# Tile 0 alone through the pooling mixer and its first routing, with tile 1's rows moved behind the first gathers, and another order of the buffer ring

## The reference

```python
# the pooling mixer of layer 1
m = multiscale_pool(h @ w_in)               # four bands of averages over the tokens, minus h
m = einsum('btgc,gce->btge', m, w_grp)      # four groups of 256 channels
y = (m * scale) @ w_out
xs = layer_norm(alpha * xs + g1 * y)        # per token; also after each expert layer

# PEER, for each block of 128 tokens ("tile"), 8 heads
q = (h @ wq).reshape(128, 8, 2, 128)
s = einsum('nhpd,hpkd->nhpk', q, keys)      # 2 x 128 scores per token and head
top_s, top_i = top_k(s, 16)                 # then the best 16 of 16 x 16 sums
gate = softmax(best_s)
act = gelu(einsum('nd,nhkd->nhk', h, u_tab[idx]))
out = einsum('nhk,nhkd->nd', gate * act, v_tab[idx])
```

## Time and profile before

| | us |
|---|---|
| median of three runs | 2215.3 (2212.99 to 2216.16) |
| the profiled execution, its own time | 2214.42 |
| its span | 2212.6 |
| PE busy | 1827.7 (83%) |
| DVE busy | 1467.5 (66%) |
| ACT busy | 882.3 (40%) |
| POOL busy | 620.3 (28%) |
| share of 16 DMA engines' span, gathers (software_dynamic) | 59.0% |
| the same, other loads (hardware_dynamic) | 22.1% |

### The profile page before, as it was taken

The page is one execution under the profiler, slowest core; times in us unless marked ns, Lnnn a source line. Parts: engine busy times, 40 slices in busy tenths (PEclk is TensorE's granted clock), DMA queues, the critical chain, the costliest instruction groups (busy, mean ns, idle before and its releaser), DMA issues.

```text
span 2212.6 us, 21909 instructions
## 1 busy us (share of the span) xinstructions
PE 1827.7 (83%) x7101; PEld 1097.5 (50%) x7101; DVE 1467.5 (66%) x3019; ACT 882.3 (40%) x2302; POOL 620.3 (28%) x567
## 2 busy tenths in 40 slices
PE   4888999899868687988877877996889888877786
PEld 3757998799656444434322333354434343322222
DVE  6767956955675666677567777525576777677755
ACT  3446433522443234344434444312343444444433
POOL 1160000000000334434354443203244344444441
PEclk9889989998988799999999999997999999999999
DMA  9754757646344599999999999845899999999995
GB/s 369 264 197 146 267 186 296 238 183 248 105 143 145 209 384 416 421 418 421 380 418 422 421 422 421 343 171 218 360 418 420 419 421 421 421 421 421 421 422 247
DMA packets 114690, 723.76 MB, mean 327 GB/s; under 512 B 11504, under 2 KB 13344, under 8 KB 34064
## 3 DMA queue, kind: packets, MB, share of 16 engines
q0 software_dynamic: 74864, 540.30, 59.0%
q1 hardware_dynamic: 39712, 182.07, 22.1%
HBM read 721.24 MB, written 1.08 MB: 326 GB/s over the span
## 4 chain that ended last, share of the span: by engine, by line
PE 40%; DMA 30%; DVE 19%; issue 5%; ACT 5%; POOL 1%; SPq 0%; DVEq 0%; ACTq 0%; POOLq 0%
DMA X<-in_k_uv,EI 15%; PE PS L2020 14%; DMA Z<-in_k_uv,EI 8%; DMA W<-in_peer_wq 5%; PE PS L1997 5%; PE PS L1709 5%; PE PS L1710 4%; PE PS L1711 4%; DVE junk L1696 4%; DVE ACC L1320 3%; DVE WL L1336 2%; PE PS L1797 2%; DMA W<-in_ada_w 2%; PE PS L2073 1%; PE PS L2035 1%
## 5 line engine op out<-in xcount | busy, mean ns | idle before, releaser
L2020 PE MATMUL PS<-X,dg 128*128 128x512 f32 x1372 | 669.1, 623 | 166.6 <-ACT dg L908 160.1
L1696 DVE CUSTOM_DVE_ANT_0 junk<-H,X 128x1024 f32<-128x1024 f32 x343 | 420.0, 1224 | 239.3 <-DMA X<-in_k_uv,EI 229.2
L899 POOL DMA_INDIRECT X<-in_k_uv,EI x343 | 377.8, 1101 | 618.8 <-PE PS L2020 375.7
L2020 PEld LDWEIGHTS PS<-X,dg 128*128 128x128 f32 x1372 | 249.0, 194 | 543.0 <-ACT dg L908 328.0
L908 ACT ACTIVATE CF<-DOT 128x1 f32<-128x1 f32 x512 | 102.2, 200 | 576.8 <-DVE DOT L1696 567.2
L2020 PE MATMUL PS<-Z,dg 128*128 128x512 f32 x504 | 248.0, 625 | 53.0 <-ACT dg L908 52.7
L908 ACT ACTIVATE dg<-CP,CG 128x128 f32<-128x128 f32 x512 | 205.7, 402 | 17.5 <-PE PS L2020 0.7
L1696 DVE CUSTOM_DVE_ANT_0 junk<-H,Z 128x1024 f32<-128x1024 f32 x126 | 154.2, 1224 | 85.7 <-DMA Z<-in_k_uv,EI 76.6
L2020 PEld LDWEIGHTS PS<-Z,dg 128*128 128x128 f32 x504 | 92.0, 195 | 191.0 <-ACT dg L908 115.9
L899 POOL DMA_INDIRECT Z<-in_k_uv,EI x126 | 137.3, 1089 | 142.4 <-PE PS L2020 122.0
L1709 PE MATMUL PS<-XH,WH 128*128 128x256 f32 x592 | 173.6, 293 | 2.4 <-ACT XH L908 1.2
(11 more groups left out here) (298 smaller groups left out, 2642.5 us busy)
## 6 DMA issues: line engine op xcount, KB each, us to landing
W<-in_ada_w SPq DMA_DIRECT2D x50, 1024.0 KB, 6.5
Y<-in_ada_w SPq DMA_DIRECT2D x22, 1024.0 KB, 5.5
W<-in_peer_wq SPq DMA_DIRECT2D x16, 1024.0 KB, 16.2
W<-in_k_ffi SPq DMA_DIRECT2D x13, 1024.0 KB, 6.6
Y<-in_k_ffi SPq DMA_DIRECT2D x9, 1024.0 KB, 5.1
W<-in_ffn_w_out SPq DMA_DIRECT2D x8, 1024.0 KB, 5.4
W<-in_k_win SPq DMA_DIRECT2D x8, 1024.0 KB, 6.1
Y<-in_k_win SPq DMA_DIRECT2D x8, 1024.0 KB, 7.5
```

The source lines that it names most:

```text
L899: e.indirect_dma_start(out=WS[k][:, :], out_offset=None, in_=I[f"k_uv{ly}"][:, :], in_offset=bass.IndirectOffsetOnAxis(ap=EI[t][:, j:j + 1 ...
L1696: e.tensor_tensor_reduce(junk, H[:, t, :], d[:, 0:D], 1.0, 0.0, ALU.mult, ALU.add, DOT[:, j:j + 1]).then_inc(v_dot, 1)
L2020: p = e.matmul(PS[:, 2 * t + q, :], dgb[n % 4][:, :], d[:, D + q * 512:D + (q + 1) * 512], start=(j == 0), stop=(j == 127))
```

## The change

The pooling bands and groups are made tile by tile, each matmul 128 tokens wide instead of 256, and bands and groups alternate. The output matmuls `po` are split by tile: tile 0's come before its `rn`, and tile 1's (`("po", 1)`) directly behind head 0's score matmuls of layer 1. Tile 1's bands and groups stand between `rn` of tile 0 and `tt` of tile 0. In both layers, `rn`, `tt` and `h` of tile 1 become three pieces of the other work that are taken after tails 0, 1 and 2 of tile 0, with a piece each. All loads of pooling weights get buffers of their own and are issued first; the keys' load no longer waits for `po`. Head 0 of tile 0 has its scores in bank 3. The twelve buffers of the gathers get another order. The diff, with its context cut to a line:

```diff
...
 MOD_SLICE = [0, 1, 2, 3, 3, 4, 5, 6, 7, 8]
-RING = list(range(2, 11)) + [13, 14, 15]
+RING = [9, 10, 4, 5, 3, 13, 2, 6, 14, 15, 7, 8]
 
...
         def chunk(i, lo, hi):
-            b = bank(high)
+            b = 4 + i if (s4, hi) == (0, 128) else bank(high)
             if hi - lo == 256:
...
                     next(h00)
-                    P("tt", ly, 1)
+                    if ly:
+                        P("po", 1)
                     yield from h00
                     P("h", ly, 0)
+                    ready.add((ly, "h"))
+                    yield
+                    P("rn", ly, 1)
+                    yield
+                    P("tt", ly, 1)
+                    yield
                     P("h", ly, 1)
-                    ready.add((ly, "h"))
+                    yield
         else:
...
 
+    def pooled(t, banks):
+
+        bands = iter(range(8))
+        for c in (0, 1):
+            P("band", next(bands), t, bank(banks))
+        for g in range(4):
+            for c in range(2):
+                c = next(bands, None)
+                if c is not None:
+                    P("band", c, t, bank(banks))
+            for c in (2 * g, 2 * g + 1):
+                P("grp", c, t, bank(banks))
+
     for ly in range(2):
-        P("rn", ly, 0)
+        if ly:
+            for i in range(4, 10):
+                P("ldp", i)
+            P("ldq", ly, 0)
+            P("ldq", ly, 1)
+            P("ldk", ly)
+            pooled(0, low)
+            P("po", 0)
+            P("rn", ly, 0)
+            pooled(1, (1, 2, 3))
+        else:
+            P("ldq", ly, 0)
+            P("ldq", ly, 1)
+            P("ldk", ly)
+            P("rn", ly, 0)
         P("tt", ly, 0)
-        P("rn", ly, 1)
-        P("ldq", ly, 0)
-        P("ldq", ly, 1)
-        P("ldk", ly)
         g = others(ly)
...
             P("sc", 1)
-            P("ldp", 4)
-            for c in range(8):
-                P("band", c, bank(low))
-            P("ldp", 5)
-            for c in range(8):
-                P("grp", c, bank(low))
-            for i in range(6, 10):
-                P("ldp", i)
-            P("po")
     P("frn", 1)
...
     last, count, where = {}, {}, {}
-    rings = {"w": [0, 1, 2, 11, 12], "q": [0, 1], "p": [2, 6, 7, 8, 9, 10], "g": RING}
+    rings = {"w": [0, 1, 2, 11, 12], "q": [0, 1], "p": [3, 13, 14, 15, 7, 8, 9, 10], "g": RING}
     turn = {k: 0 for k in rings}
...
 
-NAME = {"xp": 3, "xt": 3, "mod": 2, "modp": 2, "gq": 3, "evac": 2, "rowp": 3, "rowa": 3, "pi": 4, "pie": 3, "band": 2, "grp": 2,
+NAME = {"xp": 3, "xt": 3, "mod": 2, "modp": 2, "gq": 3, "evac": 2, "rowp": 3, "rowa": 3, "pi": 4, "pie": 3, "band": 3, "grp": 3,
         "btp": 3, "bte": 3, "pqe": 5}
...
             if a[0] < 6:
-                return (p_band, 8) if a[0] == 4 else (p_grp, 8)
+                return (p_band, 16) if a[0] == 4 else (p_grp, 16)
             return p_po, 1
...
 
+        def scores(t, h):
+            return 3 if t == h == 0 else 7
+
+
         def arena(ly):
-            return (p_part, 65) if ly == 0 else (p_po, 1)
+            return (p_part, 65) if ly == 0 else (p_band, 16)
 
...
                 elif kind == "ldk":
-                    w.wait_ge(*arena(a[0]))
+                    w.wait_ge(*((p_rt, 16) if a[0] else arena(0)))
                     e.dma_start(KK[:, :, :], I["k_keysT"][a[0]].rearrange("c k n -> k c n")).then_inc(d_k, 16)
...
                         w.wait_ge(*vacated(before))
-                    w.wait_ge(*arena(ly))
+                    w.wait_ge(p_part, 65)
+                    if ly and k in (4, 5):
+                        w.wait_ge(p_po, 1)
                     e.indirect_dma_start(out=WS[k][:, :], out_offset=None, in_=I[f"k_uv{ly}"][:, :],
...
                 elif kind == "band":
-                    c, b = a
-                    w.wait_ge(p_band, c + 1)
-                    act(mT[:, c, :], PS[:, b, 0:256], ACT.Copy).then_inc(a_band, 1)
+                    c, t, b = a
+                    w.wait_ge(p_band, 8 * t + c + 1)
+                    act(chunk(mT, c, t), PS[:, b, 0:128], ACT.Copy).then_inc(a_band, 1)
                 elif kind == "grp":
-                    c, b = a
-                    w.wait_ge(p_grp, c + 1)
-                    act(m2[:, c, :], PS[:, b, 0:256], ACT.Copy, scale=C2[:, c_psc + c:c_psc + c + 1]).then_inc(a_grp, 1)
+                    c, t, b = a
+                    w.wait_ge(p_grp, 8 * t + c + 1)
+                    act(chunk(m2, c, t), PS[:, b, 0:128], ACT.Copy, scale=C2[:, c_psc + c:c_psc + c + 1]).then_inc(a_grp, 1)
 
...
                     else:
-                        w.wait_ge(*arena(ly))
+                        w.wait_ge(*((p_po, 1) if ly else arena(0)))
                     w.wait_ge(a_row, 6 if ly == 0 else 14)
...
                         q = piece - 1
-                        s, s2 = PS[:, 7, q * 128:(q + 1) * 128], S2[:, q * 128:(q + 1) * 128]
+                        s, s2 = PS[:, scores(t, h), q * 128:(q + 1) * 128], S2[:, q * 128:(q + 1) * 128]
                         w.wait_ge(p_rt, nth("rt", ly, t, h, 0))
-                        w.wait_ge(*arena(ly))
+                        w.wait_ge(*arena(0))
                         e.max(TV[:, q, 0:8], s).then_inc(v_own, 1)
...
                     w.wait_ge(d_k, 16 * (ly + 1))
-                    take(7)
+                    b = scores(t, h)
+                    take(b)
                     for q in range(2):
                         c = 2 * h + q
-                        p = e.matmul(PS[:, 7, q * 128:(q + 1) * 128], chunk(PQ, c, t), KK[:, c, :], start=True, stop=True)
+                        p = e.matmul(PS[:, b, q * 128:(q + 1) * 128], chunk(PQ, c, t), KK[:, c, :], start=True, stop=True)
                     p.then_inc(p_rt, 1)
-                    free[7] = [(v_r7, nth("rt", ly, t, h, 2))]
+                    free[b] = [(v_r7, nth("rt", ly, t, h, 2))]
                 elif kind == "tail":
...
                 elif kind == "band":
-                    c, b = a
+                    c, t, b = a
                     d, arrived, count = slot("ldp", 4)
...
                     take(b)
-                    for t in range(2):
-                        p = e.matmul(PS[:, b, 0:256], Z[:, t, c * 128:(c + 1) * 128], bd[:, c // 2, t, :], start=(t == 0),
-                                     stop=(t == 1))
+                    for i in range(2):
+                        p = e.matmul(PS[:, b, 0:128], Z[:, i, c * 128:(c + 1) * 128],
+                                     bd[:, c // 2, i, t * 128:(t + 1) * 128], start=(i == 0), stop=(i == 1))
                     p.then_inc(p_band, 1)
-                    free[b] = [(a_band, c + 1)]
+                    free[b] = [(a_band, 8 * t + c + 1)]
                 elif kind == "grp":
-                    c, b = a
+                    c, t, b = a
                     g = c // 2
...
                     wg = d[:, :].rearrange("p (g k n) -> p g k n", g=4, k=2)
-                    w.wait_ge(a_band, 8)
+                    w.wait_ge(a_band, 8 * t + 2 * g + 2)
                     w.wait_ge(arrived, count)
...
                     for k in range(2):
-                        p = e.matmul(PS[:, b, 0:256], wg[:, g, k, (c % 2) * 128:(c % 2) * 128 + 128], mT[:, 2 * g + k, :],
-                                     start=(k == 0), stop=(k == 1))
+                        p = e.matmul(PS[:, b, 0:128], wg[:, g, k, (c % 2) * 128:(c % 2) * 128 + 128],
+                                     chunk(mT, 2 * g + k, t), start=(k == 0), stop=(k == 1))
                     p.then_inc(p_grp, 1)
-                    free[b] = [(a_grp, c + 1)]
+                    free[b] = [(a_grp, 8 * t + c + 1)]
                 elif kind == "po":
-                    w.wait_ge(a_grp, 8)
-                    for t in range(2):
-                        for j in range(2):
-                            b = 4 + 2 * t + j
-                            take(b)
-                            for i in range(8):
-                                d, arrived, count = slot("ldp", 6 + i // 2)
-                                w.wait_ge(arrived, count)
-                                p = e.matmul(PS[:, b, :], chunk(m2, i, t), by_k(d, 2)[:, i % 2, j * 512:(j + 1) * 512],
-                                             start=(i == 0), stop=(i == 7))
-                        p.then_inc(p_y if t == 0 else p_po, 1)
+                    t = a[0]
+                    for j in range(2):
+                        b = 4 + 2 * t + j
+                        take(b)
+                        for i in range(8):
+                            d, arrived, count = slot("ldp", 6 + i // 2)
+                            w.wait_ge(arrived, count)
+                            w.wait_ge(a_grp, 8 * t + i + 1)
+                            p = e.matmul(PS[:, b, :], chunk(m2, i, t), by_k(d, 2)[:, i % 2, j * 512:(j + 1) * 512],
+                                         start=(i == 0), stop=(i == 7))
+                    p.then_inc(p_y if t == 0 else p_po, 1)
 
...
```

## The result

The changed kernel takes 2254.05 us (2252.86 to 2257.53, 4 runs); the kernel before took 2214.96 on the same chip. The ratio is 1.018, with a 95% interval of 1.0162 to 1.0198: 39 us slower, against the forecast of 35 and the range of 2224 to 2262. The profiled execution took 2257.53, the longest of the four and 43 more than the one before, so steps read from the two traces add up to 43. Gather 0 of layer 0 is 1.95 us later in it; 1.93 of that is already there at tile 0's transposes (`tt`, 727.89 against 725.96), ahead of which only the place of this layer's loads in the list changed. In the six experiments that leave the way to this gather as the changed kernel or the one before has it, it lies between -1.0 and +2.2: about that much of any step is chance.

A forecast was written before the change was run, and what follows sets the result against it. The DMA was taken as the bound, other work costing time only where it runs dry. Terms 17.5 + 13.8 + 2 x 3.3 + 2.8 + 4.6 - 10.3 = +35.0 us gave 2250 us, range 2224 to 2262.

The forecast's parts named there:

- part 2: Behind the first gathers: tile 1's moved pieces delay head 1's scores; gather 16 +17.5 us in layer 0, +13.8 in layer 1.
- part 3: Later heads: shifted pieces and queries delay gather 32 by 3.3 us in each layer, gather 128 of layer 0 by 2.8.
- part 4: End of layer 0: the new buffer order puts 2 MB of loads ahead of the last gather, +4.6 us.
- part 1: From pooling to layer 1's first gather: tile 0's transposes start earlier, so gather 0 comes 10.3 us earlier.
- The rival without bubbles: Reordered TensorE work costs only its instructions, no idle: layer 0's gather 16 at +59.3 us, total 2227; chance 0.2.
- The start decides: Gathers 16 and 32 keep their distance from gather 0, only start and loads count: 2209.6 us; chance 0.08.
- The start gains nothing: Layer 1's start: slow narrow steps held by ScalarE, tile 0's transposes not before 1498: +45 us, 2260; chance 0.12.

The follow-up runs named there:

- the root's experiment: Changed kernel with `rn` of tile 0 in layer 1 behind the ninth of tile 1's sixteen band and group steps: 2251.71 us.
- late loads: Changed kernel with loads `ldp 2` and `ldp 3` also waiting for the tail of gather 252: 2249.02 us.
- three tails later: Changed kernel with tile 1's `rn`, `tt` and `h` after tails 3, 4 and 5: 2269.43 us.
- rows ahead of dot 0: Changed kernel with layer 0's earlier order and, in layer 1, tile 1's `rn`, `tt`, `h` behind head 0's indices, before all dots and tails: 2218.34 us.
- layer 0's rows back: Changed kernel with layer 0's order as in the kernel before, layer 1 as changed: 2227.63 us.
- queries first: Changed kernel with part 0's queries and heads 0 and 1's scores ahead of tail 0, both layers: 2195.79 us; with later loads and root, 2184.66 us.
- tile 0 first: Changed kernel with tile 0's queries and both heads' scores before tile 1's rows, both layers: 2216.23 us; with later loads and root, 2207.38 us.

## Why the prediction was right, step by step

| step (shift in us) | predicted | measured |
|---|---|---|
| part 2: layer 0, gather 0 to 16 | +17.5 | +19.4 |
| part 2: layer 1, gather 0 to 16 | +13.8 | +15.7 |
| part 3: to gather 32, layer 0 and 1 | +3.3 each | +4.5, +5.0 |
| part 3: gather 128 of layer 0 | +2.8 | +3.1 |
| part 4: last tail of layer 0 | +4.6 | +4.8 |
| part 1: bands to gather 0 of layer 1 | -10.3 | -12.5 |

**Part 1** was right in its mechanism, shown by the root's experiment: 12.2 us from `po` to `tt` were forecast and 12.0 came. That it came so near is partly luck: the same steps with the same pause took 10.6 us in the trace of the late loads and 13.6 in that of three tails later, by the clock behind the pause. The gain is 2.2 larger because of smaller things: tile 0's part before `rn` took 21.2 us (21.7 forecast), and from `tt` to gather 0 it was 17.5 instead of 20.15, of which I had counted only 1.3. The query matmuls stood behind a pause of 1.51 us, not 2.8, and took 3.81 us at a granted clock of 1.00 instead of 5.45 at 0.69; that term was missing.

**The narrow matmuls** go at 0.112 us each (1.79 us for 16 on the chain), half of the 0.225 of the wide ones (7.19 for 32): splitting by tile cost nothing at full clock, though each weight is loaded twice. The Trainium skill says in "TensorE: Matmul & The Clock Gate", "Part 3: Packing small matmuls", that a weight load overlaps a running matmul only when it goes to other rows of the array. For these shapes the rows contradict that: here loads and matmuls all use the full array, and both were busy side by side (PEld for 3.62 and PE for 3.81 us of 3.82, in the window of tile 0's narrow query matmuls in layer 1).

**Part 2** was right in kind and place. Tail 2 starts at +23.4 from gather 0 (22.4 to 24.1 forecast) and the scores of head 1 end at +59.4 (55.9 to 59.7). (The upper end of that range was added up wrong: 39.1, seven tails, four half queries and the scores make 58.6.) Tail 5 ends at +39.9, just past the forecast 39.1, as tails 2 and 3 together ran at 6.70 us, not 3.43: the lower clock after the pause (0.54 granted) lasted over both tails, for which the forecast's steps leave about 1 us. Gather 16 at +70.4 is 0.4 beyond the upper end given. That gather 16 of layer 1 waited for its indices in the kernel before, though the earlier trace rows name a tail, fits with VectorE's timeline: the last instruction on `EI` starts at 1572.93 and takes 0.17, and the gather goes out 0.28 after it. The rival without bubbles (+59.3) is refuted in both layers. That head 1's scores are late by the tails ahead of them is shown by the two experiments that change their number.

**Part 3** is a little low in both layers; that it hangs on the place of head 1's scores fits with the layer 1 of rows ahead of dot 0, where it is gone. Gather 128 has no experiment of its own; with layer 0's rows back the shift grows by 0.5 us from gather 32 to it, against 3.1, so it belongs to layer 0's order.

**Part 4** is shown in its mechanism, and in its size to within 2 us: 4.6 forecast, 4.8 in the trace, 4.9 in layer 0's rows back. From gather 240 to the last tail, late loads gained 3.8 us against the changed kernel, 5.2 in queries first and 6.5 in tile 0 first (with the root's repair beside them, which comes later). The loads were not ahead of the last gather, as the forecast has it, but issued behind it.

**The rivals.** "The start decides" needed head 1's scores at +38; they came at +59. "The start gains nothing" is refuted by gather 0 of layer 1. The sum of the steps is +39.9 in the trace for +35.0: every loss is low by 0.2 to 1.9 us, and the start's surplus takes 2.2 back. With 1.95 ahead of the change, 1.0 between gathers 128 and 240 and 0.3 at the end it is the 43 of the trace; the medians have 39.

## What to carry to other kernels

When gathers or loads run ahead in a ring, a late index costs nothing until the ring is empty, and then costs in full: for every reordering, find the next request that depends on it and count what every in-order engine must pass first. Work put "behind the first gathers" to shorten a start lands in front of the next indices; on ScalarE one square root or eight evacuations stop TensorE, though each is short. And a hole that is mended at gather 16 has to be looked for at gather 32: with the stock of work only moved, the time came back to that of the kernel before and no further; with all of it ahead of the first tail, where TensorE was idle, it fell below. Where the queue is full, read progress from when the data is used, not from when its gather is issued.

## What the runs showed of the hardware

- Float32 matmuls with 128 columns and their weight loads go at 0.112 us each at a granted clock of 1.00, with 256 columns at 0.216 to 0.225. At the lower level (1.2 GHz) eight narrow ones take 1.71 us on the chain and not 0.89.
- The clock behind a pause differs for the same code. Eight kernels have the same steps with the same pause of 3.39 us. PE came back at the lower level and stayed there for 2.9 us in the changed kernel, for 6.1 us in queries first and in three tails later; in late loads it came back at the full level and kept it. Without the pause (root in its place) it kept it too. Windows of the changed kernel, queries first, late loads and the root in its place, PEclk third from the end:

```profile
1516.20:1519.10 2.90, 2.88 (x13) 2.89 (x14) 0.81 (x1) 0.94 (x4) 0.00 (x0) 0.50 0.00 0
```
```profile
1482.40:1488.50 6.10, 6.07 (x28) 6.07 (x29) 0.82 (x2) 2.25 (x8) 0.00 (x0) 0.50 0.00 0
```
```profile
1509.29:1515.20 5.91, 5.91 (x53) 5.91 (x54) 0.81 (x1) 4.12 (x14) 0.00 (x0) 1.00 0.00 0
```
```profile
1512.10:1520.00 7.90, 7.88 (x70) 7.57 (x69) 5.08 (x8) 5.29 (x18) 0.00 (x0) 1.00 0.00 0
```

- 2.1 MB of weight loads, issued 1 to 3 us behind the last gather, delayed the last tail by 4.8 and 4.9 us in two traces; at 425 GB/s they take 4.9. Gathers that were issued before a load still shared the engines with it.
